# Delta rule phase: who makes the low part of z's weights, and when

## What is computed

```python
h = rmsnorm(x, ln_mix_pre)
proj = h @ w_in                                   # columns q, k, v, z, decays, gates, ...
q, k, v = silu(conv5(proj[q,k,v]))                # 5 taps over time; q and k are normalised per head
g = -exp(a_log) * softplus(a + dt_bias); beta = sigmoid(b)
# per head, chunked: S_t = exp(g_t)(I - beta_t k_t k_t^T) S_{t-1} + beta_t k_t v_t^T ;  o_t = S_t^T q_t
# inside a chunk a unit lower triangular system (I + A) is solved; then across chunks the state is passed on
o_a = rmsnorm(o_forward + o_backward, norm_a) * silu(proj[z])
```

## Time and profile before

| | |
|---|---|
| median of 3 runs | 2488.51 us (2475.11 to 2491.18) |
| the profiled execution, its own time | 2481.65 us |
| its span | 2479.9 us |
| mean granted clock of TensorE | 0.953 |
| busy: PE, PEld, DVE, ACT, POOL | 90%, 69%, 41%, 32%, 36% |
| delta rule phase | 301 to 781 us |
| L885, the low part on GpSimd | 44 instructions from `wr`, 105.7 us |
| L1179, the high part on ScalarE | 44 instructions from `wr`, 46.4 us |

### The profile page before, as it was taken

How to read it: one execution, slowest core, us unless ns; L and a number is a source line. 1 busy time by engine, 2 the same in 40 slices (tenths; PEclk the granted TensorE clock), 3 DMA queues, 4 the chain that set the end, 5 groups by cost and what they waited for, 6 DMA issues and landing times. The chain is left out here.

```text
span 2479.9 us, 30354 instructions
## 1 busy us (share of the span) xinstructions
PE 2220.9 (90%) x11597; PEld 1722.9 (69%) x11597; DVE 1017.9 (41%) x1686; ACT 788.7 (32%) x1237; POOL 881.5 (36%) x788
## 2 busy tenths in 40 slices
PE   7999897999987988999996988789999898599994
PEld 5888776777776876888875655678888687444441
DVE  3222355676753463332245554465674215311112
ACT  4333242443433434333324444222121423111110
POOL 4333146565652444444321102335444343000001
PEclk9999899999998999999997999899999999699998
DMA  5433032333323433323305302111111333799994
GB/s 163 108 77 87 11 101 73 89 93 80 88 52 97 130 128 119 101 90 96 118 17 104 80 29 82 29 30 29 23 31 22 101 91 130 297 409 423 423 423 168
DMA packets 287448, 300.30 MB, mean 121 GB/s; under 512 B 78192, under 2 KB 248432, under 8 KB 277680
## 3 DMA queue, kind: packets, MB, share of 16 engines
q1 hardware_dynamic: 278584, 266.80, 34.1%
q0 software_dynamic: 5280, 19.18, 2.1%
q10 hardware_dynamic: 3456, 12.58, 1.2%
HBM read 322.01 MB, written 26.84 MB: 141 GB/s over the span
## 5 line engine op out<-in xcount | busy, mean ns | idle before, releaser
L2607 PE MATMUL moe_bank<-ex_wgu,Y 128*64 128x512 f32 x768 | 171.0, 596 | 1.6 <-ACT Y L2654 1.6
L655 PE MATMUL gdn_bank<-hh,gdn_ws 128*128 128x512 f32 x368 | 161.1, 438 | 9.3 <-POOL gdn_ws L885 9.3
L885 POOL TENSOR_TENSOR gdn_ws<-gdn_wr,gdn_ws 128x1024 fp32r<-128x1024 f32 x44 | 105.7, 2408 | 117.4 <-ACT gdn_ws L1179 117.3
L657 PE MATMUL gdn_bank<-hh,gdn_ws 128*128 128x512 f32 x368 | 145.9, 397 | 0.0
L656 PE MATMUL gdn_bank<-hl,gdn_ws 128*128 128x512 f32 x368 | 145.3, 395 | 0.0
L2607 PEld LDWEIGHTS moe_bank<-ex_wgu,Y 128*64 128x64 f32 x768 | 66.2, 138 | 100.9 <-issue 100.9
L2579 POOL DMA_INDIRECT hT<-token_rows,rows x24 | 22.8, 951 | 304.1 <-PE moe_bank L2592 236.5
L2285 DVE TENSOR_TENSOR ff_hes<-hT,ff_hes 128x1024 fp32r<-128x1024 f32 x16 | 23.5, 1469 | 207.5 <-ACT ff_hes L2244 207.5
L655 PE MATMUL ff_bank<-ff_wds,ff_hes 128*128 128x512 f32 x256 | 99.7, 389 | 1.8 <-DVE Y L2301 1.8
L656 PE MATMUL ff_bank<-ff_wds,ff_hes 128*128 128x512 f32 x256 | 99.6, 389 | 0.0
L657 PE MATMUL ff_bank<-ff_wds,ff_hes 128*128 128x512 f32 x256 | 99.6, 389 | 0.0
(11 more groups left out here) (590 smaller groups left out, 6008.8 us busy)
## 6 DMA issues: line engine op xcount, KB each, us to landing
ex_wgu<-in_w_gate_e SPq DMA_DIRECT2D x48, 1024.0 KB, 19.1
ex_wgu<-in_w_up_e SPq DMA_DIRECT2D x48, 1024.0 KB, 18.5
ex_wd<-in_w_down_e SPq DMA_DIRECT2D x48, 1024.0 KB, 21.3
Y<-in_w_in SPq DMA_DIRECT2D x48, 512.0 KB, 3.9
gdn_wr<-in_w_in SPq DMA_DIRECT2D x44, 512.0 KB, 4.2
wu<-in_w_ff SPq DMA_DIRECT2D x16, 1024.0 KB, 11.7
ff_wd<-in_w_ff SPq DMA_DIRECT2D x16, 1024.0 KB
expert_rows<-Y ACTq DMA_DIRECT2D x24, 512.0 KB
```

What stands on the lines that cost most here:

```text
L655: pe.matmul(bank, left(0, l), right(0, r), start=(start and n == 0), stop=False)
L657: ins = pe.matmul(bank, left(1, l), right(0, r), start=False, stop=(stop and n == len(pairs) - 1))
L885: pool.tensor_tensor(ws[:, r % 2, 1], raw[r], ws[:, r % 2, 0], ALU.subtract).then_inc(s.lo, 1)
L2607: ins = pe.matmul(bank[2 + j][half, :], hgT[:, j, k, half], w[:, e, k], start=(k == 0), stop=(k == KT - 1))
```

## The change

The low part of z's weights, for the six heads g = 2 to 7, is made by VectorE instead of GpSimd, in two halves of four slices each (128x512). The first half (`low_z(g, 0)`) stands in VectorE's chain after the second convolution place of step 0, the second (`low_z(g, 1)`) after the first convolution place of step 1. The first half waits for the high part, the second raises a new semaphore z_lo. Whoever waited for lo of a block now asks `lowered(r)`, which gives z_lo for those six blocks and lo, with the count less the z blocks so far, for the others. These are TensorE at a block's first slice and SP before the load two blocks on. GpSimd leaves out those six blocks.

```diff
+        z_lo = ph.sem("z_lo")
...
+        def by_vector(r):
+            g, b = place_of(r)
+            return b == 4 and g >= 2
+
+        def lowered(r):
+
+            n = sum(by_vector(a) for a in range(r + 1))
+            return (z_lo, n) if by_vector(r) else (s.lo, r + 1 - n)
...
-                sp.wait_ge(s.lo, r - 1)
+                sp.wait_ge(*lowered(r - 2))
...
             def lower(r):
-                if r < nblocks:
+                if r < nblocks and not by_vector(r):
...
-                        pe.wait_ge(s.lo, r + 1)
+                        pe.wait_ge(*lowered(r))
...
-            def chain(i):
+            def low_z(g, part):
+                if g is None or g < 2:
+                    return
+                r = 5 * g + 3
+                ks = slice(part * KT // 2, (part + 1) * KT // 2)
+                if part == 0:
+                    dve.wait_ge(s.hi, r + 1)
+                ins = dve.tensor_tensor(ws[:, r % 2, 1, ks], raw[r][:, ks], ws[:, r % 2, 0, ks], ALU.subtract)
+                if part == 1:
+                    ins.then_inc(z_lo, 1)
+
+            def chain(i, g):
...
                         convolve(1)
+                        if st == 1:
+                            low_z(g, 1)
...
                         convolve(1)
+                        if st == 0:
+                            low_z(g, 0)
...
-                    chain(i)
+                    chain(i, g)
```

## The result

The changed kernel takes 2494.96 us (median of 13 runs, 2487.6 to 2498.89) against 2485.16 us (13 runs) of the kernel before: ratio 1.0038, 95% interval 1.0027 to 1.005, that is 6.7 to 12.4 us more. Its profiled execution took 2493.5 us, span 2491.6; against that of before this is 11.7 us of span.

A forecast was written before the change was run, and what follows sets the result against it. The period was taken as bound by a loop through TensorE, the inversion, SP, the weights' DMA, ScalarE and kT. -0.5 + 4.1 = +3.6 us gave 2485.3 or 2492.1 by base, told as 2489, range 2474 to 2500.

The forecast's parts named there:

- The stall is not in the loop: TensorE's 1.5 us z stall lies outside the period's loop; removed, it moves to the wait for kT, winning 0.5 us.
- The port lengthens the inversion: VectorE's two halves, with two SBUF operands each, stretch GpSimd's inversion by 0.35 us each, 0.69 us a period.
- The upper bound of 1.38: GpSimd's inversion is blocked for the full length of both VectorE halves: 1.38 us a period, 8.3 in all.
- It is paid for in the period: The longer inversion delays SP, the weights' DMA, ScalarE and kT by 0.69 us; six periods, +4.1 us.
- rival 4: TensorE's idle becomes one of over 3 us and its granted clock drops; 30 us lost, 2515 us; chance 0.02.
- the one fall I had quoted: Clock drop to 1.2 GHz in a 10 us window ahead of the first period, in which TensorE worked 2.72.
- The number: Whole kernel: +3.6 us, told as 2489 us, range 2474 to 2500, within 1% at 0.97.
- rival 3: The port blocks GpSimd's inversion in full, 1.38 us a period: +7.8 us, 2489.4 (2496.3 on the median); chance 0.13.
- VectorE's halves at no cost: The two added subtractions, 8.4 us of VectorE, fit into idle time ahead of R and S: cost 0.
- GpSimd's next low part: Block 19's low part, now directly behind the inversion, gains 0.3 us that no one waits for: cost 0.

The follow-up runs named there:

- the pair of runs with two operands and with one: Two: the port alone. One: the same, but the two added VectorE instructions are maxima with one SBUF operand; 2483.27 us, a single execution.
- the port alone: Kernel before, GpSimd still making z's low part, plus two unused VectorE subtractions of 128x512 with two SBUF operands at the change's places; 2491.89 us, ratio 1.0028.
- where the inversion closes the loop: Load and decays early, with z's low part for g = 2 to 7 left out on every engine; 2465.44 us, ratio 0.9931.
- the first two experiments: First: changed kernel with z's low part for g = 2 to 7 left out on every engine, 2487.2 us, ratio 1.0004. Second: the port alone.
- load and decays early: Changed kernel, SP's load of block 5g+5 ahead of the wait for the inversion, VectorE's eight decays ahead of the first product's mask; 2474.47 us, ratio 0.9952.

## Why the prediction was right, and where its size was off

- **The stall is not in the loop: right.** -0.5 us was forecast for six stalls of 1.5. With the stall alone removed the time is the same (1.0004), and the wait for kT is 2.56 us where 2.7 was forecast. In the changed kernel it is 2.1 to 2.4 us up to 661 us, less than the 2.5 to 3.5 of the forecast, because some of the idle stands ahead of the first product with the inverse (1.05 us at 490.59).
- **The port lengthens the inversion: right, and a little too small.** 0.69 us was taken, 0.8 to 1.0 measured; a half costs 0.32 to 0.54 us. The prediction's 0.35 for each came from a subtraction with 2.35 us for a low part that takes 2.40 in the earlier trace rows, and was carried over to instructions that fall elsewhere in GpSimd's rhythm. The upper bound of 1.38 wasn't reached, but not because GpSimd is held for less: it is held to the end of VectorE's instruction. The bound left out that GpSimd's instruction starts up to 0.14 us later and that half of its own 0.29 us passes meanwhile. Cause shown by the pair of runs with two operands and with one, and by the tap.
- **It is paid for in the period: right in the direction, and smaller.** Of 0.8 and 1.0 us the two undisturbed periods show 0.33 (52.07 for 51.74) and 0.56. The rest was regained between SP and ScalarE: from the load's issue to the high part 3.8 and 4.0 us (488.95 to 492.94) instead of 4.1 and 4.4 (488.72 to 493.11). Why the load lands sooner I haven't tested. Six periods at this rate are 2 to 3.4 us, for +3.6 forecast. With the port alone one period shows the whole 0.82, and 0.85 a period are paid where the inversion closes the loop.
- **The step that failed is rival 4.** I gave it 0.02 and priced it at 10 us of low clock a period, the one fall I had quoted, and held against it that TensorE had been idle more than twice as long there (7.3 of 10 us). By the prediction's own list a granted clock under 1.00 between 450 and 700 us was the sign of rival 4, and it came in four periods. The falls are short, 3.4 us, and cost 1.5 us of TensorE's time: 4 x 1.5 = 6 us up to 715 us. The other 3.4 of the 9.45 measured are left for the port, at the upper end of the 2 to 3.4 above. It should have been a term of 1.5 us a period with a fair chance, since the forecast itself made the waits longer than any that the trace of before had shown with the clock holding.
- **The number: right by its allowances, and so in part by luck.** +9.4 us by the ratio for +3.6 forecast is within 1% and in the stated range. But it is more than the +7.8 of rival 3, the most that any case but rival 4 allowed. From the median of 13 runs of the kernel before, 2485.16, that would have been 2493.0. 2494.96 us lies in the range through a base of three runs that was 3.3 us higher (2488.51) and through the few us that were added for the runs' spread.
- **VectorE's halves at no cost: right.** R starts directly behind the first half, and S still waits 0.98 us for TensorE.
- **GpSimd's next low part: right.** It starts at 479.94, as soon as ScalarE's high part is there, and no one waits for it.

Still open: when a wait is followed by a fall. In the changed kernel and in the first two experiments, between 400 and 705 us, all ten falls stood directly behind a single wait of 2.2 us or more: seven for kT (2.21 to 2.56 us), three for z's weights (2.26 to 2.50). None came behind 2.1 or less; the longest there in the kernel before is 1.84. But not every long wait has one. Of the 16 waits of 2.2 us or more in these three runs six had none: 2.48, 2.45 and 2.39 us in the first experiment, 2.28, 2.26 and 2.26 in the second. And past 705 us the line at 2.2 doesn't hold: one wait for VectorE's mask (L1340 of the kernel before) was followed directly by a fall in the changed kernel (1.87 us at 723.71, 8 us behind a wait of 2.97) and with load and decays early (1.84 at 709.74, 9 us behind one of 0.47), and by none in the kernel before (1.86 at 715.61). What tells these apart I haven't tried, and each kernel has one trace.

## What to carry to other kernels

Ahead of removing a stall of the busiest engine, follow the loop that returns to the same instruction one period later; a stall outside it comes back as a wait at the loop's closing point, and what was paid for its removal is a loss. A resource freed earlier pays only if the queue that was ordered around its lateness is reordered too: here one DMA issue and eight decays, moved on top of the change, turned +0.4% into -0.5%, and did nothing without it. Before a VectorE instruction with two SBUF operands is put beside GpSimd, look whether GpSimd is in the loop; with one operand in SBUF it cost nothing here.

## What the hardware showed beyond that

TensorE's clock fell to the lower level in or behind single waits of 1.8 to 2.9 us, although TensorE was busy 93% of a period of the changed kernel (48.73 of 52.48). Most falls lasted 3.4 us and cost 1.5 us of TensorE's time; where it then waited less for another engine, less of that reached the period (53.08 us with a fall and 52.56 without in the run with the port alone).

A GpSimd instruction that met a VectorE one with two SBUF operands ended 0.13 to 0.16 us behind it, whether it had started 0.14 us behind it (0.70 us long) or together with it (0.83). So what the meeting costs depends on the start by some tenths, and 0.01 to 0.02 us decided which of the two was held.

A VectorE instruction can also be the one that is held. With the decays ahead, kT starts 0.13 us behind GpSimd's low part and takes 2.79 us instead of 0.69. The timeline of the run with load and decays ahead:

```profile
495.81 2.37 POOL L898 TENSOR_TENSOR gdn_ws<-gdn_wr,gdn_ws 128x1024 fp32r<-128x1024 f32 x1
495.94 2.79 DVE L1371 TENSOR_TENSOR gdn_kT<-gdn_cv,gdn_rn 128x512 f32<-128x512 f32 x1 [0.77 <-ACT gdn_rn L1251]
```
